# Conditioning products inside the RWKV-7 loop, and a whole gate conditioned beside the first projection

## The reference, cut to what matters

```python
def _ada(c, w, b):
    mod = jax.nn.silu(c) @ w + b              # (1, 2048) @ (2048, 6144)
    shift, scale, gate = jnp.split(mod[:, None, :], 3, axis=-1)
    return shift, scale, gate

for i in range(2):
    shift, scale, gate = _ada(c, ada_w[i, 0], ada_b[i, 0])
    h = x * (1.0 + scale) + shift
    y = mixer_ab(h, ...) if i == 0 else mixer_c(h, ...)
    x = layer_norm(ALPHA * x + (1.0 + gate) * y, ...)
    shift, scale, gate = _ada(c, ada_w[i, 1], ada_b[i, 1])
    h = x * (1.0 + scale) + shift
    x = layer_norm(ALPHA * x + (1.0 + gate) * swiglu(h), ...)
```

## Time and profile before

| | us |
|---|---|
| median of 3 runs (2922.16 to 2932.91) | 2932.14 |
| the profiled execution: its own time | 2923.16 |
| the profiled execution: span of the trace | 2920.9 |
| PE busy in the span | 2759.6 (94%) |
| DVE, ACT, POOL busy in the span | 1943.6, 1184.5, 271.5 |
| first projection (stage 2) in the trace | 45 to 348 |
| RWKV loop up to the end of step 7 | 348 to 790 |
| output projection | 849 to 944 |

### The profile page before, as it was taken

One profiled execution on the slowest core, in us unless ns is written; L12 is line 12 of the kernel. 1 busy time (PEld: TensorE's weight loads), 2 busy tenths in 40 slices (PEclk: granted clock), 3 DMA queues, 4 the chain that ended last, 5 costly groups with the idle time before them and its releaser, 6 DMA issues. The chain is left out here.

```text
span 2920.9 us, 42283 instructions
## 1 busy us (share of the span) xinstructions
PE 2759.6 (94%) x17774; PEld 2311.4 (79%) x17774; DVE 1943.6 (67%) x1885; ACT 1184.5 (41%) x1373; POOL 271.5 (9%) x199
## 2 busy tenths in 40 slices
PE   3999889999989999999999979999999999999996
PEld 3888788888867788888888868888877888888885
DVE  5778624444558688888888788776477855555557
ACT  2555423333443433333333434546443333333332
POOL 0000000000000400000000019363022000000000
PEclk9999968999899899999999989999999999999998
DMA  8888533332147588888888737664548755555552
GB/s 309 296 293 306 195 95 92 88 86 79 31 176 285 212 312 308 331 306 331 308 312 324 276 115 245 245 232 144 200 164 332 279 191 186 187 190 193 192 187 87
DMA packets 320856, 636.70 MB, mean 218 GB/s; under 512 B 10606, under 2 KB 82980, under 8 KB 304708
## 3 DMA queue, kind: packets, MB, share of 16 engines
q1 hardware_dynamic: 314546, 621.84, 60.8%
q10 hardware_dynamic: 6162, 12.72, 1.2%
HBM read 632.42 MB, written 2.10 MB: 217 GB/s over the span
## 5 line engine op out<-in xcount | busy, mean ns | idle before, releaser
L531 DVE TENSOR_TENSOR s_wl<-s_raw,s_wh 128x2048 fp32r<-128x2048 f32 (+1 forms) x393 | 913.9, 2326 | 516.2 <-ACT s_wh L526 507.1
L526 ACT ACTIVATE s_wh<-s_raw 128x2048 fp32r<-128x2048 f32 x396 | 758.4, 1915 | 1084.6 <-PE pa L726 419.4
L724 PE MATMUL pa<-s_wh,s_hth 128*128 128x512 f32 x1312 | 527.6, 402 | 13.7 <-DVE s_wl L531 8.5
L725 PE MATMUL pa<-s_wl,s_hth 128*128 128x512 f32 x1312 | 517.3, 394 | 0.0
L726 PE MATMUL pa<-s_wh,s_htl 128*128 128x512 f32 x1312 | 516.9, 394 | 0.0
L724 PEld LDWEIGHTS pa<-s_wh,s_hth 128*128 128x128 f32 x1312 | 249.8, 190 | 75.4 <-DVE s_wl L531 13.1
L726 PEld LDWEIGHTS pa<-s_wh,s_htl 128*128 128x128 f32 x1312 | 250.0, 191 | 53.6
L725 PEld LDWEIGHTS pa<-s_wl,s_hth 128*128 128x128 f32 x1312 | 250.3, 191 | 48.7
L724 PE MATMUL pb<-s_wh,s_hth 128*128 128x512 f32 x704 | 274.5, 390 | 0.0
L726 PE MATMUL pb<-s_wh,s_htl 128*128 128x512 f32 x704 | 274.2, 389 | 0.0
L725 PE MATMUL pb<-s_wl,s_hth 128*128 128x512 f32 x704 | 274.2, 389 | 0.0
(11 more groups left out here) (396 smaller groups left out, 3756.3 us busy)
## 6 DMA issues: line engine op xcount, KB each, us to landing
s_raw<-in_ffn_w_in SPq DMA_DIRECT2D x176, 1024.0 KB, 5.3
s_adaw<-in_ada_w SPq DMA_DIRECT2D x144, 1024.0 KB, 6.1
s_raw<-in_ffn_w_out SPq DMA_DIRECT2D x88, 1024.0 KB, 8.1
s_raw<-in_ab_w_in SPq DMA_DIRECT2D x48, 1024.0 KB, 8.8
s_raw<-in_diff_w_in SPq DMA_DIRECT2D x48, 1024.0 KB, 5.2
s_adaw<-in_ada_w SPq DMA_DIRECT2D x48, 512.0 KB, 5.5
s_raw<-in_ab_w_out SPq DMA_DIRECT2D x16, 1024.0 KB, 9.8
s_qkv<-in_ada_w SPq DMA_DIRECT2D x16, 1024.0 KB, 7.2
```

The costliest lines, as they stand in the source:

```text
L526: act.activation(wh[:, s % 2, :, 0:width], raw[:, s, :, 0:width], ACT.Copy).then_inc(hi_done, 1)
L531: dve.tensor_tensor(wl[:, s % 2, :, 0:width], raw[:, s, :, 0:width], wh[:, s % 2, :, 0:width].bitcast(F32), ALU.subtract).then_inc(lo_done, 1)
L724: pe.matmul(o, a_hi, w_hi, start=start and k == 0, stop=False)
L725: pe.matmul(o, a_hi, w_lo, start=False, stop=False)
```

## The change

The 32 blocks of 128 columns become 32 rows of blocks: `adaw` is loaded with 128 x 2048 weights of one row block (`parts[1, c, k]`, 8 KB pieces), and `row_products` multiplies it with four matmuls, each with 32 equal columns of `silu_c[:, k]` as the stationary operand and 512 weights as the streamed one, into 32 partitions each of the bank `ROWS` (`pa[:, 0]`). 16 row blocks add up to the shift, 16 to the scale of sub-layer 1. `ROWS_IN` places them: 2 and 6 in steps -2 and -1, then 4, 4, 2, 4, 4, 4, 2, one at a time at three places in front of `level_q(t, 2)`, `(t, 3)`, `(t, 4)` and one at the end of the step. After each 16, ACT copies the bank to `wide`, PE transposes it (4 transposes), DVE adds the bias: in step 2 and in step 7. The gate of sub-layer 0 is now whole in stage 2: 16 loads and 32 DVE operations, at 16 units, of which 8 loads are new; the places are 13, 14, 24, 26, 27, 37, 39, 40 for its first half and 43 to 50 for its second. Stage 5 has no conditioning any more.

```diff
-        OUT_STEPS = ((1, 0), (1, 1), (1, 3), (2, 0), (2, 1), (2, 3), (3, 0), (3, 1))
-        LOAD_AT = [ABC * s + 2 + i for s in range(3) for i in range(PAIR_LOADS)] + [3 * ABC + 1 + i for i in range(PAIR_LOADS)]
-        BURSTS_IN = {-2: 1, -1: 3, 0: 4, 1: 4, 2: 4, 3: 4, 4: 3, 5: 3, 6: 3, 7: 3}
+        EARLY = sorted([(ABC * s + 2 + i, s + 1, i) for s in range(3) for i in range(8)]
+                       + [(q, 4, i) for i, q in enumerate((13, 14, 24, 26, 27, 37, 39, 40))]
+                       + [(q, 5, i) for i, q in enumerate(range(43, 51))])
+        ROW_LOADS = 32
+        ROWS_IN = {-2: 2, -1: 6, 0: 4, 1: 4, 2: 2, 3: 4, 4: 4, 5: 4, 6: 2}
...
+        def row_load(sp, b):
+
             if b < 2:
-                sp.wait_ge(ada_step, JOB_STEPS + 2 * (n - 1))
+                sp.wait_ge(ada_step, JOB_STEPS + 2 * (len(EARLY) + b - 1))
             else:
-                sp.wait_ge(burst_done, 2 * (b - 1))
-            src = ada_w.rearrange("a b (k p) n -> (a b) p k n", p=P)[m, :, :, at:at + P]
+                sp.wait_ge(rows_done, b - 1)
+            sp.dma_start(adaw[:, b % 2], parts[1, b // KT, b % KT]).then_inc(wide_in[b % 2], 16)
...
-            for k in range(half * KT // 2, (half + 1) * KT // 2):
-                mm = pe.matmul(col, block[:, k], silu_c[:, k:k + 1], start=(k == half * KT // 2),
-                               stop=(k == (half + 1) * KT // 2 - 1), skip_group_check=True)
+            for j in range(4):
+                mm = pe.matmul(ROWS[32 * j:32 * j + 32], silu_c[:, k:k + 1].to_broadcast((P, 32)), adaw[:, b % 2, j * W:(j + 1) * W],
+                               start=(k == 0), stop=(k == KT - 1), skip_group_check=True)
+            mm.then_inc(rows_done, 1)
+
+        def rows_copy(act, m):
+
+            act.wait_ge(rows_done, KT * m + KT)
+            act.activation(wide[:, 0:W], ROWS, ACT.Copy).then_inc(rows_copied, 1)
+
+        def rows_turn(pe, m):
+
+            pe.wait_ge(rows_copied, m + 1)
+            for j in range(4):
+                mm = pe.transpose(ROWS[:, j * P:(j + 1) * P], wide[:, j * P:(j + 1) * P], ident)
+            mm.then_inc(rows_turned, 1)
...
                 if lev:
-                    bursts(t, 0)
+                    rows_at(t, 0)
                     level_q(t, 2)
                 if chain:
                     chain_x(c, 1)
-                if lev:
-                    bursts(t, 1)
...
-            half_cols(pe, 4, TAIL_STEPS + 2 * PAIR_LOADS)
```

More of the change, by code:

```diff
@@ L579, in part_step, with early_step, early_cols @@
                                          ALU.add).then_inc(ada_step, 1)
[L581 to L589, removed]
+        def early_step(dve, n):
+            q, g, i = EARLY[n]
+            dve.wait_ge(wide_in[n % 2], sum(32 if EARLY[m][1] < 4 else 16 for m in range(n % 2, n + 1, 2)))
             for kk in range(2):
-                frm, to, k = adaw[:, n % 2, kk * D // 2:(kk + 1) * D // 2], wide[:, 0:D // 2], 2 * i + kk
+                frm, k = adaw[:, n % 2, kk * D // 2:(kk + 1) * D // 2], 2 * i + kk
+                to = wide[:, 0:D // 2] if g < 4 else wide[:, D // 2:D]
                 if k == 0:
-                    dve.wait_ge(ada_cols, len(JOBS) + (n // PAIR_LOADS if n < BURST_LOADS else 4))
+                    dve.wait_ge(ada_cols, len(JOBS) + {1: 0, 2: 1, 3: 2, 4: 0, 5: 4}[g])
                     dve.tensor_scalar(to, frm, silu_c[:, 0:1], None, ALU.mult).then_inc(ada_step, 1)
                 else:
-                    dve.wait_ge(ada_step, at + kk)
+                    dve.wait_ge(ada_step, JOB_STEPS + 2 * n + kk)
                     dve.scalar_tensor_tensor(to, frm, silu_c[:, k:k + 1], to, ALU.mult, ALU.add).then_inc(ada_step, 1)
[L599 to L604, removed]
+        def early_cols(pe, g):
+            last = max(n for n in range(len(EARLY)) if EARLY[n][1] == g)
+            pe.wait_ge(ada_step, JOB_STEPS + 2 * last + 2)
+            pe.wait_ge(ada_out, len(JOBS) + g - 1)
+            at = 0 if g < 4 else D // 2
+            for j in range(8):
+                mm = pe.matmul(pt[:, 1, j:j + 1], wide[:, at + j * P:at + (j + 1) * P], ones[:, 0:1], start=(j == 0), stop=True,
                                skip_group_check=True)
@@ L1664, in _ @@
                     gla_gate_act()
+                if t in (2, PAIRS - 1):
+                    rows_copy(act, 0 if t == 2 else 1)
                 if lev:
@@ L2448, in _ @@
                 if s < 3 and m == ABC - 4:
-                    half_cols(pe, s, JOB_STEPS + 2 * PAIR_LOADS * (s + 1))
+                    early_cols(pe, s + 1)
                 if s < 3 and m == ABC - 3:
@@ L2452, in _ @@
                     turn_pe(pe, 0, range(2 * s + 2, 2 * s + 4))
-                if q == FIRST_UNITS - 3:
-                    half_cols(pe, 3, TAIL_STEPS)
+                if q in (41, FIRST_UNITS - 1):
+                    early_cols(pe, 4 if q == 41 else 5)
             pe.wait_ge(z0_out, FIRST_UNITS)
@@ L2767, in gla_turn_out, with rows_at @@
                 mm.then_inc(g_oT, 1)
-            halves = [(b, half) for b in range(BURSTS) for half in range(2)]
-            def bursts(t, at):
-                first_half = 2 * sum(BURSTS_IN[i] for i in range(-2, t))
-                if lev and at < 6:
-                    mine = (at,)
-                elif lev:
-                    mine = range(6, 2 * BURSTS_IN[t])
+            def rows_at(t, at):
+                if t not in ROWS_IN:
+                    if t == PAIRS - 1 and at == 1:
+                        rows_turn(pe, 1)
+                    return
+                b = sum(ROWS_IN[i] for i in range(-2, t))
+                if t < 0:
+                    mine = range(ROWS_IN[t]) if at == 3 else ()
+                elif t == 2:
+                    if at == 0:
+                        rows_turn(pe, 0)
+                    mine = (at - 2,) if at >= 2 else ()
                 else:
-                    mine = range(2 * BURSTS_IN[t]) if at == 6 else ()
+                    mine = (at,) if at < ROWS_IN[t] else ()
                 for i in mine:
-                    burst(pe, *halves[first_half + i])
+                    row_products(pe, b + i)
             for t in range(-2, PAIRS + 1):
```

133 lines of the change are left out of this document (53 added, 80 removed).

## The result

The changed kernel takes 2816.99 us (median of 4 executions, 2812.17 to 2823.79), the kernel before 2932.52 beside it (4, 2922.16 to 2938.1): ratio 0.9612, 95% interval 0.9578 to 0.9645. Between the two profiled executions the difference is 2923.16 - 2823.79 = 99.4 us.

A forecast was written before the change was run, and what follows sets the result against it. PE was taken as the bound, with the conditioning bursts on its path in the loop. Loop -92 and first projection +2 make -90: 2833 from the profiled 2923.2, 2842 for a median; range 2822 to 2880.

The forecast's parts named there:

- The base step: RWKV loop: one step without conditioning takes 33.8 us, derived from steps 5 and 6 without their half bursts.
- The new wait ahead of `scores`: RWKV loop, each step: PE newly waits 1.0 us for DVE's row of factors once the half burst ahead is gone.
- The first projection: Stage before the loop: added DVE operations, transfers and column sums cost +2 us, bounds 0 and 21.
- the two pushed boundaries: First projection: loads at 26, 27, 39 and 40 delay the next `low`, about 0.5 us at each of two boundaries.
- Partial overlap: Rows in the loop: column groups overlap only in part, 2.4 us a row or 1.9 with pairs; 2866 to 2879; chance 0.17.
- no overlap: Rows in the loop: the column groups don't overlap at all, 3.7 us a row; 2914; chance 0.06.
- the case at 1.2 GHz: Rows run one after another with the gate at 1.2 GHz, 7.4 us a row; slower, about 3030; chance 0.03.
- turn to DVE: First projection becomes bound by DVE or transfers, the added 21 us fully seen; 2863; chance 0.11.
- It does nothing: RWKV loop: no gain, because ACT and DVE bound each level anyway; rejected, with no separate chance listed.
- Step 0: First full loop step, 46.2 us: loses 14.9 of bursts, gains four rows, a 1.0 wait and 0.7; -9.2.
- Steps -2 and -1: Ahead of step 0: eight rows, four waiting for their transfers, replace eight halves at 1.2 GHz; -2 us.
- Step 7: Loop's last step: six halves (16.2) go, 5 lost to DVE's logits, 5 regained by clock; -16, unknown by 6.

The follow-up runs named there:

- the shrunken rows: Changed kernel with conditioning rows from the ninth on (except the second sum's first) cut to one product over 16 columns, loads and waits kept: 2798.11 us.
- both moves: Changed kernel with rows placed at TensorE's waits (chain U, V ahead of level 5, factors) and four rows shifted from ahead of step 0 into later steps: 2786.42 us, ratio 0.9516.

## Why the forecast came out low

**Right, by the forecast's own steps.** The row: 1.0 us forecast, 1.00 in the timeline and 0.99 by the shrunken rows. The base step: 33.8 forecast, 33.7 measured. The new wait ahead of `scores`: 1.0 forecast, 0.87. So a step with four rows came to 37.6 for 37.8, steps 1 to 4 to -51.7 for -50.3. The output projection: from the last copy of V to the end the profiled executions differ by 100.2 - 99.4 = 0.8 us, for 0, and less than the 3.6 us between two executions of the kernel after. The reason given holds as well: without the column sums (16 records, 1.8 us) PE's wait for DVE's statistics behind the projection (L760) is 4.9 us instead of 3.4. The first projection: the lora transposes start 2.15 us later (351.32 for 349.17) for 2, though the reason was partly another: by the run without the gate's pieces the two pushed boundaries that made up 1.0 of it are not there, the column sums account for 0.7, and the rest is spread of the stage's end. That the sum came to 2 is luck. ACT's copy and DVE's store of the two sums cost nothing that a step shows: step 2 with two rows and the transposes took 36.05 for 36.4. Rows wait for their loads only ahead of step 0, and the clock is 1.00 in steps 1 to 6, both as said.

**The rivals.** Partial overlap (1.9 to 2.4 us a row) is what two groups give, not four; no overlap would have been 3.55, and the run with one group shows it as 2883, its rows at a clock of 1.00, so that serial rows alone don't make the case at 1.2 GHz. The prediction lets that case decide "from roughly 3.8 us a row on"; by its own figures (90 us gained at 1.0 us a row, 72 of them lost by 2.7 us more) it would be 4.4, and the run with one group, at 3.55, is indeed still 50 us faster than before. The Trainium skill ("TensorE: Matmul & The Clock Gate", Part 3) says that matmuls start and end strictly in program order; had the two records of each matmul been kept together by that, a row would have been 2.4. The trace has it otherwise. In the row at 568.34 four records start within 20 ns, at 568.343, .349, .356 and .363, and four more 0.45 us after them, from 568.795 to .815: two turns of four. As no two records start together in the run with one group, the four of a turn are of four groups, one of each matmul. The records don't name their matmul, so in what order the program holds them, and with it whether the skill's rule of order is broken, isn't shown. The Trainium skill's 2.38 times for three groups (same section), carried over to four as an estimate, would have given 1.17; here four groups give 3.55 / 1.00 = 3.55 times, and two 1.93. The first projection did not turn to DVE. "It does nothing" falls with the clock and the step times.

**Wrong: what the removed work cost at 1.2 GHz outside steps 1 to 5.** The terms that were mis-sized, against the profiled execution after:

- *Step 0*, forecast -9.2, measured -15.1. The step counted six half bursts at 1.88 us, though the granted clock of the earlier trace rows for steps 0 to 3 was 0.89 and that of step 0 alone 0.79; the bursts' own price there was 16.1 for 14.9 (one half took 3.14), and the rest of the step's work came back to 2.4 GHz too, for which the forecast had counted nothing here, though it had counted 5 us of it for step 7. The run with the bursts cut shows -17.2 in this step. This is 5.9 of the 9.4 us that the two profiled executions differ beyond the forecast.
- *Steps -2 and -1*, forecast -2, measured -4.7: 2.7 us. The rows themselves came out nearly as said: the six in step -1 take 18.7 us, from 384.63 to the transposes behind them at 403.34, for 19, and the two ahead of them 3.3 for 3.8. The other 1.8 us are the work between the two groups, 17.9 us instead of 19.7: the clock of these steps rose from 0.57 to 0.68, and the forecast had counted only the rows. (Its "all at 1.2 GHz" was not quite so either: the granted clock was 0.50 in the two halves and 0.57 in the six.) What bounds the rows, two buffers and a load behind the row before the last, was right: four rows wait for their loads, 9.1 us, and in the run with four rows less there is no such wait and step 0 starts 18.5 us earlier (384.4 against 402.9).
- *Step 6*, forecast 35.8, measured 33.9. The base was the mean of steps 5 and 6 of before, and step 6 has no transposes and decays of a later pair (10 records less, 1.6 us in a full step after); before, a clock of 0.96 in it had made up for them. In step 5 the miss is 0.2.
- *Step 7* went the other way, -14.2 for -16, at a clock of 0.88; in the run with four rows less it is 25.2 us at 1.00, which would be -17. The bound of 6 either way held.

These are 5.9 + 2.7 + 1.9 + 0.2 - 1.8 = 8.9; with 1.4 from steps 1 to 4, and -0.8 and -0.15 for the end and the first projection, they make the 9.4.

**Wrong: the range, for a second reason.** It took the change against one execution and moved it by 9 us to the median; it allowed nothing for the two kernels' own spread. The profiled execution before was 9.36 us under its median and the one after 6.80 over its own: 99.37 + 9.36 + 6.80 = 115.53. Measured again, the difference is 108.8, with the same ratio within its interval (0.9629 for 0.9612). So the forecast of -90 was too small by 19 to 26, of which 9 are in the steps above. The rest is what executions of one kernel differ by: the medians of before in four sets of executions are 2932.5, 2934.4, 2926.4 and 2924.6, those of after 2817.0 and 2815.8. For the kernel after the two profiles put 4.5 us of it ahead of the last copy of V and 3.6 behind it. Where the kernel before loses its 9 us between the profiled execution and the median was not followed, so the cause of this part stays open.

**Where the gain comes from.** One step at a time: with the rows in one group the kernel takes 2883.5, some 50 us under the median of before beside it (2934.4). In a full step that form costs about what the bursts did (a row 3.55, a burst 3.76 at 2.4 GHz). By the two profiles it gains 17.2 us in steps 1 to 6, where it has 20 rows for 21 bursts and a clock of 1.00 for 0.89 to 1.00, 7.0 in step 0, 15.8 in step 7, which has no rows (42.1 to 26.4 us), and loses 4.8 ahead of step 0: 35.2 by the last copy of V. The other 15 lie behind it and in the spread of executions. A second group gives 48 more, the third and fourth 19 (single executions, from different sets).

## What to carry to other kernels

When small products with one useful row of output have to share TensorE with a chain of work, stream the long operand, and give each slice its own column group: the price falls with the number of turns. Then place each piece where the engine waits for another one, since a piece ahead of ready work costs its whole length (1.0 us) and four pieces moved into waits of 0.6 to 0.9 gave back 0.5 to 0.9 each (steps of 35.4 to 34.0 us instead of 37.6), and put none where it waits for its own load. When an engine is freed of filler in a stretch below full clock, count the rest of the stretch at the higher clock as well, step by step, and give the range the spread of both kernels.

## What the runs showed of the hardware

- Eight fp32 records of 512 columns and 32 output rows: 3.55 us in one column group, 1.84 in two, 1.00 in four, at a granted clock of 1.00. The two records of a matmul run in different turns, and the matmuls of different groups share a turn.
- The granted clock in steps 1 to 4 was 0.89 to 0.95 with bursts and 1.00 with rows, also in the run with the rows in one group, whose steps are as long (PE busy for 43.8 of 47.8 us).
- PE stopped for 0.3 to 1.5 us inside the loop on "issue", mostly inside groups of 64x64 records: 1.2 us once in the run with rows in waits, 3.2 us in four stops with both moves, 0.5 with four rows less, and 1.7 in two stops in the kernel before with its bursts cut, which has no rows at all. So rows close behind the chain's products are not what it takes. What PE waited for there is open; it wasn't tried.
